# The opening of a hybrid attention and convolution layer: seven weight blocks as float32 on SP's queue, cast on chip

## The reference

```python
hn = rmsnorm(x, norm_g)
q, k, v, z_a, hc, gb, gc, z_b, g = split(hn @ w_in)          # 3x1536, 512, 4x512, 2048 columns
attn = merge_by_denominators([banded_attention(q[i], k[i], v[i], dilation=d)
                              for i, d in enumerate((1, 4, 16))])   # +-64 keys each
a = (silu(z_a) * attn) @ w_attn_out
c = (silu(z_b) * (gb * conv3(gc * hc))) @ w_conv_out
g_a, g_c = split(sigmoid(g + b_gate))
y = rmsnorm(x + (g_a * a + g_c * c) @ w_o, final_g)
```

## Time and profile before

| | us |
|---|---|
| median of 3 runs (lowest, highest) | 1551.26 (1548.31, 1553.46) |
| span of the profiled execution (core 1, its slowest) | 1567.8 |
| spans of its other cores | 1537.5 to 1566.9 |
| PE busy, share of the span | 1508.7, 96% |
| DVE, ACT, POOL busy | 859.2, 706.3, 189.9 |
| bytes moved by DMA | 125.5 MB |

### The profile page before, as it was taken

How to read it: one execution, slowest core, us unless ns; L and a number is a source line. 1 busy time by engine, 2 the same in 40 slices (tenths; PEclk the granted TensorE clock), 3 DMA queues, 4 the chain that set the end, 5 groups by cost and what they waited for, 6 DMA issues and landing times.

```text
span 1567.8 us, 31208 instructions; the slowest of 8 cores (1537.5 to 1567.8 us)
## 1 busy us (share of the span) xinstructions
PE 1508.7 (96%) x13640; PEld 884.4 (56%) x13640; DVE 859.2 (55%) x1113; ACT 706.3 (45%) x1063; POOL 189.9 (12%) x364
## 2 busy tenths in 40 slices
PE   6889999999999999999999999999999999999997
PEld 5545676565565544444444777767676544444443
DVE  4555146328337469744447545648375597544355
ACT  4665445546556432433333356657565321222222
POOL 3232000000000011211113100000001100000011
PEclk9977889999999999999999999999999999999999
DMA  8573013212222243533468623233233142222156
GB/s 197 140 169 81 19 38 72 36 38 58 46 65 37 37 75 55 127 68 66 79 154 257 162 35 79 29 71 53 56 46 48 19 72 47 41 41 41 20 182 248
DMA packets 57065, 125.50 MB, mean 80 GB/s; under 512 B 16481, under 2 KB 16609, under 8 KB 56930
## 3 DMA queue, kind: packets, MB, share of 16 engines
q0 software_dynamic: 25344, 46.15, 20.4%
q1 hardware_dynamic: 31586, 77.37, 16.4%
HBM read 145.97 MB, written 23.66 MB: 108 GB/s over the span
## 4 chain that ended last, share of the span: by engine, by line
PE 88%; DMA 6%; DVE 3%; ACT 1%; issue 1%; POOL 1%; SPq 0%; POOLq 0%; ACTq 0%; DVEq 0%
PE ps L442 79%; PE ps L454 8%; DMA Y<-xw 5%; DMA wbf<-wblk 1%; DVE Y L406 1%; PE ps L469 1%; DVE Y L397 1%; ACT Y L393 1%; DVE Y L430 0%; POOL stat L589 0%; ACT Y L429 0%; ACT hnT L429 0%; POOL wbf L473 0%; SPq L473 0%; DVE hnT L430 0%
## 5 line engine op out<-in xcount | busy, mean ns | idle before, releaser
L442 PE MATMUL ps<-hnT,wbf 128*128 128x512 bf16 (+5 forms) x5776 | 1048.1, 339 | 20.4 <-DVE Y L430 4.4
L442 PEld LDWEIGHTS ps<-hnT,wbf 128*128 128x128 bf16 x5776 | 530.9, 99 | 469.8 <-issue 47.0
L429 ACT ACTIVATE Y<-ps 128x512 bf16<-128x512 f32 (+5 forms) x369 | 220.3, 603 | 282.1 <-PE ps L442 264.7
L393 ACT ACTIVATE Y<-ps 128x1024 bf16<-128x1024 f32 (+2 forms) x296 | 242.1, 863 | 195.5 <-PE ps L442 131.2
L397 DVE TENSOR_TENSOR Y<-ps,Y 128x512 f32<-128x512 f32 (+1 forms) x200 | 126.4, 664 | 298.2 <-PE ps L454 259.1
L406 DVE SCALAR_TENSOR_TENSOR Y<-Y,ps 128x512 f32<-128x512 f32 x192 | 131.3, 685 | 213.5 <-PE ps L442 154.3
L473 POOL DMA_DIRECT2D wbf<-wblk x160 | 89.9, 565 | 928.3 <-PE ps L442 814.4
L393 ACT ACTIVATE Y<-ps,cf 128x512 f32<-128x512 f32 x128 | 87.1, 685 | 189.0 <-PE ps L442 181.9
L393 ACT ACTIVATE Y<-Y 128x1024 bf16<-128x1024 f32 x80 | 84.4, 1055 | 153.7 <-DVE Y L406 85.2
L397 DVE TENSOR_TENSOR Y<-Y,et 128x1024 bf16<-128x1024 bf16 x192 | 130.6, 686 | 9.1 <-ACT Y L393 4.2
L454 PEld LDWEIGHTS ps<-Y 64*128 64x128 bf16 x4640 | 116.4, 95 | 31.0 <-issue 23.8
(11 more groups left out here) (25 smaller groups left out, 444.0 us busy)
## 6 DMA issues: line engine op xcount, KB each, us to landing
wbf<-wblk POOLq DMA_DIRECT2D x160, 256.0 KB, 5.4
Y<-xw SPq DMA_DIRECT2D x56, 512.0 KB, 5.9
y<-Y SPq DMA_DIRECT2D x32, 512.0 KB, 4.1
Y<-xw SPq DMA_DIRECT2D x48, 256.0 KB, 4.8
Y<-wblk POOLq DMA_DIRECT2D x16, 256.0 KB, 6.2
et<-etab SPq DMA_DIRECT2D x8, 384.0 KB, 6.8
cv<-Y SPq DMA_DIRECT2D x4, 768.0 KB, 7.0
Y<-cv SPq DMA_DIRECT2D x4, 768.0 KB, 4.8
```

The source lines that it names most:

```text
L393: R.add("act", [lambda e: e.activation(out=out.a, in_=in_.a, func=func, scale=scale, **kw)], c_act(in_.n) + (0.2 if accum is not None else ...
L429: return e.activation(out=out.a, in_=in_.a, func=AF.Copy)
L442: fns = [(lambda e, m=m: e.matmul(m[0].a, lhsT=m[1].a, rhs=m[2].a, start=m[3], stop=m[4])) for m in mms]
```

## The change

The weight blocks of the first two groups no longer go through `wload`. A new `wblock` brings each as float32 by SP's queue into a landing buffer and casts it into its slot on DVE or ACT, whichever the planner chooses. The seven transfers are recorded between the token tiles, in the order v, k, q, hc, gc, zb, gb. The landing buffers become a ring of nine for blocks and own tokens together; the halo tiles keep the first four. There are three buffers of normalised tokens instead of two. The planner's transfer time of a token tile becomes 1.9 us. All of the first eight tiles are recorded ahead of chunk 0 instead of four. `one` moves to another address, as the ring takes its place. At the end 36 matmuls of 128 columns and 15 of 512, on strided views of `hnT`, write PSUM bank 0; nothing reads them.

```diff
--- before.py
+++ after.py
@@ -360,8 +360,10 @@
         tgcV = [yb(66 + 4 * i, 2048, F32) for i in range(2)]
         woV = yb(72, 16384, BF16)
         gb0 = yb(0, 4096, F32)
-        xt0 = [yb(k, 4096, F32) for k in (4, 8, 12, 20)]
-        xn0 = [yb(24 + 2 * i, 2048, BF16) for i in range(2)]
+        land = [yb(k, 4096, F32) for k in (4, 8, 12, 20, 84, 88, 92, 96, 100)]
+        landc = {"i": 0}
+        xt0 = land[:4]
+        xn0 = [yb(k, 2048, BF16) for k in (24, 26, 30)]
         jk0 = yb(28, 2048, BF16)
         gb1 = yb(88, 4096, F32)
         xt1 = [yb(92 + 4 * i, 4096, F32) for i in range(3)]
@@ -542,6 +544,17 @@
                 o = wbf.cols(s * 1024, 1024)
                 dma("pool", o.a, src, list(after), [o], 1.7)
 
+        def next_land():
+            landc["i"] += 1
+            return land[(landc["i"] - 1) % len(land)]
+
+        def wblock(k, j):
+
+            col, s = seq[k][j], wslot(k, j)
+            f = next_land().cols(0, 1024)
+            dma("sp", f.a, bass.AP(wblk, (col // 128) * 128 * 1024, [[1024, 128], [1, 1024]]), [], [f], 1.9)
+            copy(wbf.cols(s * 1024, 1024), f, ("dve", "act"), dcost=0.65)
+
         def wslot(k, j):
             assert wst["i"] > k
             return 4 * (k % 2) + PLACE.get(k, range(4))[j]
@@ -600,7 +613,7 @@
             for row0, dims, p0, np_ in loads:
                 o = xt.cols(0, 1024, p0, np_)
                 dma("sp", o.a, bass.AP(xw, row0 * D, [[st * D, n] for st, n in dims] + [[1, D]]), [], [o],
-                    1.7 * np_ / 128)
+                    1.9 * np_ / 128)
             x_all, n_all = xt.cols(0, 1024), xn.cols(0, 1024)
             rs = rms_stat(x_all, junk.cols(0, 1024))
             stt(n_all, x_all, rs, gb.cols(0, 1024), ALU.mult, ALU.mult)
@@ -616,7 +629,7 @@
         def ln_own(p, bank):
 
             ln_tile([(16 * 64 + R16[p], [(16, 128)], 0, 128)], [(p * 256 + 64, [[1, 128]], 0, [[1, 128]])],
-                    xt0, xn0, gb0, jk0, bank)
+                    [next_land()], xn0, gb0, jk0, bank)
 
         def ln_span(c, i0s, n, bank):
 
@@ -1108,7 +1121,7 @@
         R.tag = "start"
         ring["r"] = (0, 1, 4, 5, 6, 7)
 
-        grow, one = yb(80, 4096, F32), yb(84, 512, F32)
+        grow, one = yb(80, 4096, F32), yb(104, 512, F32)
         g_in, ones = grow.cols(0, 1024, 0, 1), one.cols(0, 128, 0, 1)
         dma("sp", g_in.a, bass.AP(gvec, 0, [[D, 1], [1, D]]), [], [g_in], 0.1)
         dma("sp", ident.a, bass.AP(cbf_d, 384, [[512, 128], [1, 128]]), [], [ident], 0.2)
@@ -1117,8 +1130,7 @@
             b = bankv[6 + j].cols(0, 512)
             pe([(b, ones, grow.cols(512 * j, 512, 0, 1), True, True, 128)], [b])
             copy(gb0.cols(512 * j, 512), b, "act")
-        wload(0)
-        wload(1)
+        wst["i"] = 2
         bcount = {"i": 0}
 
         def ln_bank():
@@ -1126,8 +1138,14 @@
             return 2 + bcount["i"] % 2
 
         R.add("dve", [lambda e: e.memset(cf.cols(CF_MH, 1).a, -0.5)], 0.1, [], [cf.cols(CF_MH, 1)])
+        first = [(0, 2), (0, 1), (0, 0), (1, 0), (1, 1), (1, 3), (1, 2)]
         for p in range(4):
             ln_own(p, ln_bank())
+            wblock(*first[p])
+        for p in range(4, 7):
+            wblock(*first[p])
+            ln_own(p, ln_bank())
+        ln_own(7, ln_bank())
         f_in, pat_in = cf.cols(CF_CW, 32), cbf.cols(0, 384)
         dma("sp", f_in.a, cfp_d.ap(), [], [f_in], 0.2)
         dma("sp", pat_in.a, bass.AP(cbf_d, 0, [[512, 128], [1, 384]]), [], [pat_in], 0.3)
@@ -1139,7 +1157,7 @@
         for c in range(4):
             R.tag = "start%d" % c
             for p in range(4 * c, 4 * c + 4):
-                if c:
+                if c > 1:
                     ln_own(p, ln_bank())
             for f in chunks[c]:
                 f()
@@ -1186,6 +1204,14 @@
             else:
                 for p in range(16):
                     out_tile(h, p, 2 * (p % 4))
+        R.tag = "probe"
+        b = bankv[0]
+        lhs = [(1, 128), (4, 128), (16, 128)]
+        mms = [(b.cols(0, 128), hnT.ap(0, [[st, 128]]), hnT.cols(2048, 128), True, True, 128)
+               for st, _ in lhs for _ in range(12)]
+        for dims in ([[1, 512]], [[4, 512]], [[16, 128], [1, 4]], [[1, 4], [16, 128]], [[4, 128], [1, 4]]):
+            mms += [(b.cols(0, 512), hnT.cols(2048, 128), hnT.ap(0, dims), True, True, 128) for _ in range(3)]
+        pe(mms, [b.cols(0, 512)])
         R.tag = ""
 
         order = R.schedule(400)
```

## The result

The changed kernel takes 1542.93 us (median of seven runs, lowest 1539.09) where the kernel before took 1551.26 on the same chip (1548.31 lowest): a ratio of 0.9943, interval 0.9923 to 0.9963. That is 8.3 us less by the medians; 12 were forecast. (Executions in which one die ran slower as a whole are left out of every ratio here, so a ratio need not be that of two medians.) A second series of the same kernel gave 0.9933 (0.9919 to 0.9946).

What follows compares the result with a forecast made beforehand. TensorE bounds 300 to 1500 us; gain lies only in its 30.6 us idle before 140. Lead 15.4 at equal clocks, less 2.4 for casts and about 1 for late tiles: 12, so 1551.3 - 12 = 1539 us, range 1528 to 1553.

Steps and rivals of the forecast that it cites:

- The way, the transfers and the first product: Opening: first tile no longer shares engines with seven blocks; 1.77 us per transfer; first product at 12.5 instead of 16.53.
- the prediction's own signs of being wrong: Opening: transfer over 2.2 us, casts over 1, chunk 2 after 53, early 0.81 on all cores, last product after last store's issue.
- chunk 2 begins at 46.3: Opening, TensorE: behind 28.2 us stand 14.5 us of product groups and 3.6 us of transposes for eight tiles, then chunk 2.
- the 72.7 of the sum: Opening, TensorE: chunk 3's end, from chunk 2 12.3, four transposes 1.8, chunk 3 12.3; before it was 89.95.
- I charged half of the casts: Opening, VectorE and ScalarE: seven casts at 0.69 us, 4.8 in all, of which 2.4 us are on the path.
- casts hold tokens up in a planned order that the real loads don't follow: Opening: one ground for the lead being waited away; 4 us of gain remain, 1547 us; chance 0.18.
- The halo stage: 90 to 140 us: sixteen halo tiles through four buffers, loads shifting with TensorE; effect taken as 0.
- The bounds (-9 to +6): 90 to 140 us: minus 9 us if these gaps close too, plus 6 if half the lead is waited away.
- The rival of the clock: Gapless TensorE work brings 0.81 at once, held to 240 us on every run's slowest core: 8 us more, 1559; chance 0.08.
- The end: After the last output tile: unused products take 5.3 us, 10.7 at double, hidden beside 11.2 us of normalisation and store; 0.
- four times: Kernel's end: far bound with products at four times 512-column time, 21 us in all, 10 us of them exposed.

Runs made afterwards that it cites:

- ring_only: Changed kernel without the unused products, weight blocks again by POOL's converting loads, nine landing buffers kept: 0.9945 of the kernel before.
- cast_dve: Changed kernel without the unused products, all seven weight conversions on VectorE: 0.9952 of the kernel before.
- no_products: Changed kernel without the 51 unused products at the end, control for the other runs: 0.9936 of the kernel before.
- xn_seven: Changed kernel without the unused products, seven buffers for normalised own tokens instead of three: 0.9921 of the kernel before.
- tiles_ahead: Changed kernel without the unused products, tiles of chunks 2 and 3 recorded one chunk earlier: 0.9918 of the kernel before.
- the halves: Changed kernel without unused products, either blocks by POOL with nine landing buffers (0.9945) or blocks by SP with five own buffers, tiles keeping four (0.9934).

## Why the prediction was right, and where its sizes were off

*The way, the transfers and the first product* were right. A transfer takes 1.74 us (1.77 taken). The first product comes at 12.2 to 14.3 over the cores (12.5 taken) because its block no longer shares the engines with six others (with POOL's loads, in ring_only, it comes at 16.8). The two terms behind that 12.5 were each off, in opposite directions: ScalarE first works on tile 0 at 7.7 us in the median (6.3 taken as its landing; 9.0 before), and its first product follows 5.3 us later and not 6.2. No wait of TensorE for a block over 0.4 us is left. But two of the prediction's own signs of being wrong came: casts over 1 us (1.06) and chunk 2 later than 53 (53.1 in the median).

*The step that failed is "chunk 2 begins at 46.3".* It begins at 53.92 on core 6 (53.1 in the median). The 7.6 us can be placed in the rows of the timeline. By 28.2 us, 141 products of chunk 0 were done (16, 32 and 40 before 25.05, then 53 at 7.51 / 128 = 0.0587 us each) and not the 192 that I took: I let all groups run as soon as their block was there, but tile 3 stood transposed only at 25.9, and the first 48 products took 0.11 to 0.12 us each (16 in 1.89, then 32 in 3.59), as the earlier trace rows already had it for the first 16. That is 51 products, 3.0 us. A gap of 0.67 us stands at 34.13. And the last transposes took 5.6 us (48.28 to 53.92), for five tiles with waits between them, instead of 1.8 for four without: 3.8 us more. Sum 7.5. Behind it the transposes ahead of chunk 3 took 3.4 us instead of 1.8, and chunk 2 took 2.5 longer than I took, so chunk 3 ends 11.7 us behind the 72.7 of the sum, which had set only 3.4 aside for casts and late tiles.

*The cause of the last and largest piece* is shown in part. The kernel before has the gap between chunks 1 and 2 as well (5.7 us in the median, 5.6 in the change); I let it close, and the change does not touch it. It is not the casts' own price: I charged half of the casts, and they were dearer than taken (1.06 instead of 0.69), but cast_dve, with 0.686, has the gap of no_products. Nor is it the number of buffers for normalised tiles alone (xn_seven). Recording the tiles one chunk earlier (tiles_ahead) brings the gap from 5.6 to 2.6 us, so the planned order makes at least that part, and it is the one edit that moved chunk 3's end, by 5 us. Chunk 2's start it moved by only 1 us. In that run's profile the last normalisations ahead of chunk 2 still wait for their statistics, whose squares stand behind copies out of PSUM on ScalarE; no run changed that, so the rest of the cause stays open. This comes nearest to the rival "casts hold tokens up in a planned order that the real loads don't follow", with the difference that products and copies out of PSUM, not casts, stand ahead of the tiles. About half of the lead was lost, so 1542.93 lies between that rival's 1547 and the forecast's 1539.

*Then the clock cost a little.* Chunk 2 took 14.80 us on core 6 instead of the 12.26 that I took (13.3 in the median over the cores). Granted clock of two pieces, core 6:

```profile
48.00:54.00 6.00, 3.32 (x46) 2.81 (x44) 5.24 (x6) 4.92 (x9) 2.96 (x6) 0.85 0.13 44
54.00:58.50 4.50, 4.50 (x13) 1.60 (x11) 3.34 (x4) 1.00 (x3) 2.23 (x4) 0.50 0.75 143
```

TensorE had worked 3.3 of the 6 us before; then it ran at the lower of its two levels, 0.50 (1.2 GHz), for 4.5 us, and chunk 2 took 2.5 us longer. The kernel before had lost 1.9 us in its chunk 3, which the forecast took off, so against that the lead shrank by 0.6. In ring_only, where the five transposes follow each other with gaps of at most 0.67 us, chunk 2 takes 12.26; in tiles_ahead the granted clock is 1.00 through chunks 2 and 3 on all eight cores, and both together take 25.7 us instead of 30.2 (medians). By these runs the late tiles cost twice, in waits and in clock.

*The halo stage* was taken at 0, and for the change it came near that: 5.4 us of lead before it, 5.1 behind it (4.9 and 3.7 without the two cores of the kernel before at 0.81). The bounds (-9 to +6) were right to be wide, as the halves show (34.9 to 40.6 us for the stage). That SP's wait for buffers would fall under 40 us and TensorE's idle time under 20 was wrong (64.2 and 27.1). TensorE's idle time to 140 us, in medians over the cores, is 28.1 us in the change, 24.2 with the tiles ahead and 19.7 without the halo loads as well, so late tiles and halo loads each hold a part of it.

*The rival of the clock* at 0.81 did not come: from 140 to 240 us core 6 has 1.00, as core 2 had before. The Trainium skill (TensorE: Matmul & The Clock Gate, "Seeing it yourself") has a limit of 13/16 on a die once three of its cores run dense matmuls. This execution does not show it: all eight cores have a granted 1.00 from 140 to 1500 us, so here the measurement decides; 0.81 stands on single cores of other executions, as in the earlier trace rows.

*The end* is hidden, as forecast.

*What is not placed.* The profiles show a lead of 5.8 us at burst 17 (4.4 without the two cores at 0.81), the medians of the runs 8.3. Part of the rest may lie in the dense part: from 500 to 1500 us TensorE idles 13.8 us in the kernel before (median over cores, 1000 less the busy time of the stretches) and 11.2 in the change, but the cores of the kernel before alone range from 8.7 to 16.1. Why, and whether it is more than the scatter of one execution each, no experiment here told. The total therefore came nearer to the forecast than the lead at chunk 3's end did (5.4 where 12 were forecast): the time was right partly by an item that the sum didn't have, which is luck.

## What to carry to other kernels

When transfers are sped up, look at once at the in-order queues of the engines that handle what has landed: here three normalised tiles waited for their transposes behind a chunk's last products, and recording the tiles a chunk earlier was worth as much at chunk 3's end as the whole change (5.3 and 5.4 us). Two gains ahead of a stage with loads of its own needn't add: measure each half alone, and what both halves share, before crediting either. Before a landing buffer is added, look at what else lives there and when it is last read: the run with two more buffers was slower than the one without.

## What the runs showed of the hardware that was not expected

The stride of a moving operand costs TensorE time. The 15 products at the end read 512 columns of hnT in five patterns, three products each, in this order: contiguous; stride 4; runs of 4 neighbours every 16 elements; stride 16; runs of 4 neighbours every 4. The weight load of a product starts when the product before it starts, so the distances of the loads are the products' durations (weight loads of core 6, granted clock 1.00):

```profile
1530.92 0.12 PEld L444 LDWEIGHTS ps<-hnT 128*128 128x128 bf16 x1 [0.34 <-issue]
1531.37 0.12 PEld L444 LDWEIGHTS ps<-hnT 128*128 128x128 bf16 x1 [0.34 <-issue]
1531.83 0.81 PEld L444 LDWEIGHTS ps<-hnT 128*128 128x128 bf16 x4 [0.34 <-issue]
1533.43 0.12 PEld L444 LDWEIGHTS ps<-hnT 128*128 128x128 bf16 x1 [0.80 <-issue]
1534.35 0.12 PEld L444 LDWEIGHTS ps<-hnT 128*128 128x128 bf16 x1 [0.80 <-issue]
1535.27 0.33 PEld L444 LDWEIGHTS ps<-hnT 128*128 128x128 bf16 x2 [0.80 <-issue]
```

A load's 0.12 us and the idle time before the next (in brackets) make a distance: three of 0.46 us, up to 1530.92, 1531.37 and 1531.83, are the stride of 4, and three of 0.92, up to 1533.43, 1534.35 and 1535.27, the stride of 16; the four loads from 1531.83, 0.81 us together, are 0.23 apart. So a stride of 4 elements doubles a 512-column product and one of 16 takes four times as long, while runs of four neighbours cost nothing. The 36 products with 128 columns ahead of them (in the row from 1527.75) have weights that lie contiguous, at stride 4 and at stride 16, twelve each; single products start 0.056, 0.056 and 0.062 us apart. So a stride of the weights shows next to no price. The Trainium skill (SBUF — State Buffer, "Door 1: The DMA port swizzle") lets bf16 operands stride up to 8 elements at full bandwidth; these rows show twice the time at 4 already, so for this operand the measurement decides. That "four times" stood in the prediction as a far bound for all 15; it is real for three.
